# Lower halves of the feed-forward down weights: a negated cast on ScalarE and an accumulating DMA in place of VectorE's subtraction

## What is computed

```python
D_FF = 2816
def swiglu(h, w_gate, w_up, w_down):
    return (jax.nn.silu(h @ w_gate) * (h @ w_up)) @ w_down
# second block, each of two layers
h = rms_norm(x, ffn1_norm[layer])
x = x + FFN_RES * swiglu(h, ffn1_w_gate[layer], ffn1_w_up[layer], ffn1_w_down[layer])
...
h = rms_norm(x, ffn2_norm[layer])
x = x + FFN_RES * swiglu(h, ffn2_w_gate[layer], ffn2_w_up[layer], ffn2_w_down[layer])
# third block
h = layer_norm(DEEPNORM_ALPHA * h + 0.5 * swiglu_3(h, ffn1_w_gate, ffn1_w_up, ffn1_w_down), ln1_g, ln1_b)
```

## Time and profile before

| | us |
|---|---|
| three runs | 3847.56, 3848.74, 3849.88 |
| median | 3848.74 |
| span of the profiled execution | 3845.6 |
| PE busy | 3347.3 |
| DVE busy | 2220.4 |
| ACT busy | 1078.6 |
| POOL busy | 1030.5 |

### The profile page before, as it was taken

The page is one execution under the profiler, slowest core; times in us unless marked ns, Lnnn a source line. Parts: engine busy times, 40 slices in busy tenths (PEclk is TensorE's granted clock), DMA queues, the critical chain, the costliest instruction groups (busy, mean ns, idle before and its releaser), DMA issues. The chain is left out here.

```text
span 3845.6 us, 39174 instructions
## 1 busy us (share of the span) xinstructions
PE 3347.3 (87%) x14474; PEld 2392.3 (62%) x14474; DVE 2220.4 (58%) x3763; ACT 1078.6 (28%) x1659; POOL 1030.5 (27%) x1092
## 2 busy tenths in 40 slices
PE   6997577778997567778999999999999999999998
PEld 4773222224774222223888888887788888887887
DVE  5678766645559766654646555547545435554644
ACT  0212111111212111111434444434443412434342
POOL 0027777764016777775000000000000000200000
PEclk9899899999899899999999999999999999999999
DMA  9459999999738999999652455543455534243453
GB/s 364 173 213 374 409 409 409 409 409 363 269 145 331 409 409 409 409 409 368 201 189 83 143 187 174 186 149 110 153 186 170 186 130 135 87 154 126 150 191 115
DMA packets 402059, 951.47 MB, mean 247 GB/s; under 512 B 30652, under 2 KB 171488, under 8 KB 401632
## 3 DMA queue, kind: packets, MB, share of 16 engines
q0 software_dynamic: 147456, 536.94, 35.5%
q1 hardware_dynamic: 245088, 397.09, 30.9%
q10 hardware_dynamic: 9344, 15.22, 1.1%
HBM read 948.06 MB, written 1.07 MB: 247 GB/s over the span
## 5 line engine op out<-in xcount | busy, mean ns | idle before, releaser
L1505 PE MATMUL PS<-v_rows,xn 128*128 128x512 f32 x1944 | 911.8, 614 | 358.7 <-DMA v_rows<-in_peer_v_dram,peer_ids 351.6
L1505 PEld LDWEIGHTS PS<-v_rows,xn 128*128 128x128 f32 x1944 | 357.8, 194 | 911.5 <-issue 566.7
L1587 DVE CUSTOM_DVE_ANT_0 u_rows<-u_rows,PS 128x1024 f32<-128x1024 f32 x512 | 622.3, 1221 | 367.7 <-DMA u_rows<-in_peer_u_dram,peer_ids 339.3
L796 DVE TENSOR_TENSOR ring_lo<-ring,ring_hi 128x2048 fp32r<-128x2048 f32 x198 | 453.0, 2293 | 260.2 <-ACT ring_hi L735 259.8
L1661 POOL DMA_INDIRECT u_rows<-in_peer_u_dram,peer_ids x512 | 483.6, 945 | 268.3 <-issue 146.1
L1661 POOL DMA_INDIRECT v_rows<-in_peer_v_dram,peer_ids x512 | 487.7, 953 | 169.3 <-issue 142.5
L735 ACT CAST ring_hi<-ring 128x2048 fp32r<-128x2048 f32 x198 | 376.9, 1913 | 245.6 <-PE PS L649 156.3
L649 PE MATMUL PS<-ring_hi,hT_hi 128*128 128x512 f32 x1056 | 418.0, 396 | 5.9 <-DVE hT_lo L830 4.6
L649 PE MATMUL PS<-ring_hi,hT_lo 128*128 128x512 f32 x1056 | 412.4, 391 | 0.0
L649 PE MATMUL PS<-ring_lo,hT_hi 128*128 128x512 f32 x1056 | 412.0, 390 | 0.0
L1565 ACT ACTIVATE xn<-cst,xn 128x128 f32<-128x128 f32 x486 | 161.5, 391 | 725.0 <-PE PS L1505 677.0
(11 more groups left out here) (434 smaller groups left out, 4403.6 us busy)
## 6 DMA issues: line engine op xcount, KB each, us to landing
ring<-in_ffn_w_gate_dram SPq DMA_DIRECT2D x132, 512.0 KB, 4.0
ring<-in_ffn_w_up_dram SPq DMA_DIRECT2D x132, 512.0 KB, 5.0
ring<-in_ffn_w_down_dram SPq DMA_DIRECT2D x66, 1024.0 KB, 4.9
ring<-in_w_in_dram SPq DMA_DIRECT2D x64, 1024.0 KB, 5.1
ada_ring<-in_ada_w_dram SPq DMA_DIRECT2D x96, 512.0 KB, 8.8
ring<-in_peer_wq_dram SPq DMA_DIRECT2D x16, 1024.0 KB, 8.1
ring<-in_c_w_in_dram SPq DMA_DIRECT2D x14, 1024.0 KB, 5.0
ring<-in_w_out_dram SPq DMA_DIRECT2D x8, 1024.0 KB, 12.0
```

The lines of the kernel that those rows point to most:

```text
L796: nc.vector.tensor_tensor(halves(c)[1], slot, halves(c)[0], ALU.subtract).then_inc(S.w_lo, 1)
L1505: ins = nc.tensor.matmul(self.PS[:, 2 * b + h, :], diag[:, r % NDIAG, :], rowsV[:, m % VRING, h * BANK:(h + 1) * BANK], start=(n % (slots ...
L1587: ins = nc.vector.tensor_tensor_reduce(rowsU[:, m % URING, :], rowsU[:, m % URING, :], H[b], 1.0, 0.0, ALU.mult, ALU.add, dots[:, e:e + 1])
```

## The change

The lower half of a down chunk is no longer made by DVE. ACT, right after the cast of the upper half, writes the negated value, rounded to fp32r, into the slot of `ring_lo`. GpSimd then issues a DMA that adds the landed float32 chunk to that slot; the sum is the value minus its upper half. PE waits for that DMA by one of two semaphores, for even and for odd steps. The lower halves of the up chunks stay with DVE and count on a semaphore of their own (`up_lo`; `ups(c)` is the number of up chunks before chunk `c`). In plain stages GpSimd does the power of the norm first and then the eleven DMAs; in stages with a layer norm the eleven DMAs come first.

```diff
+            def ups(c):
+                return c if c < 2 else 2 + (c - 2) // 3 * 2 + (c - 2) % 3
             def up(pe, c, i, parity, half, head=False):
-                pe.wait_ge(S.w_lo, count(c + 1, i, 3 * WINDOWS))
+                pe.wait_ge(S.up_lo, count(ups(c) + 1, i, 2 * WINDOWS))
...
             def down(pe, s, c, i, first=False):
-                pe.wait_ge(S.w_lo, count(c + 1, i, 3 * WINDOWS))
+                pe.wait_ge(down_odd if s % 2 else down_even, count(16 * (s // 2 + 1), i, 8 * WINDOWS))
                 pe.wait_ge(S.hid_lo, count(s + 1, i, WINDOWS))
...
                     nc.scalar.copy(halves(c)[0], self.ring[:, (base + c) % RING, :]).then_inc(S.w_hi, 1)
+                    if c == last or c > 2 and c % 3 == 1:
+                        nc.scalar.activation(halves(c)[1], self.ring[:, (base + c) % RING, :], ACT.Copy, scale=-1.0).then_inc(S.down_neg, 1)
...
-                    nc.vector.tensor_tensor(halves(c)[1], slot, halves(c)[0], ALU.subtract).then_inc(S.w_lo, 1)
+                    nc.vector.tensor_tensor(halves(c)[1], slot, halves(c)[0], ALU.subtract).then_inc(S.up_lo, 1)
...
-                    for c in (3 * s + 4, 3 * s + 5):
-                        if c <= last:
-                            lo(c, i)
+                    if 3 * s + 5 < last:
+                        lo(3 * s + 5, i)
...
             def _(pool):
+                if not layer_norm:
+                    self.norm_gpsimd(pool, S)
+                for s in range(FF_STEPS):
+                    c = min(3 * s + 4, last)
+                    pool.wait_ge(S.down_neg, s + 1)
+                    nc.gpsimd.dma_start(halves(c)[1], self.ring[:, (base + c) % RING, :], accum_op=ALU.add).then_inc(
+                        down_odd if s % 2 else down_even, 16)
                 if layer_norm:
                     self.layer_norm_gpsimd(pool, S)
-                else:
-                    self.norm_gpsimd(pool, S)
```

More of the change, by code:

```diff
@@ L619, in ffn @@
         with ExitStack() as ctx, self.stage(
-                "n_ms n_rstd n_tr hT_hi hT_split w_hi w_lo silu_done hid_ready hid_turned hid_hi hid_lo first_out l_mu l_ms l_rstd", name) as (block, S):
+                "n_ms n_rstd n_tr hT_hi hT_split w_hi up_lo down_neg silu_done hid_ready hid_turned hid_hi hid_lo first_out l_mu l_ms l_rstd", name) as (block, S):
             silu = self.sb("silu_gate", [P, NB, FF_COLS], ctx=ctx)
@@ L629, in ffn @@
             WINDOWS = 4
+            down_even, down_odd = (nc.alloc_semaphore(f"down_lo_{parity}_{name}") for parity in ("even", "odd"))
             if layer_norm:
```

## The result

The changed kernel takes **3865.65 us** (median of 6 runs, 3860.01 to 3875.79), the kernel before 3848.34 us beside it (6 runs, 3841.62 to 3853.78): a ratio of **1.0049, 95% interval 1.0034 to 1.0064**. It is slower by 17 us, more than twice the 0.2% that a measurement here can tell from no change. The profiled execution took 3860.01 us, the shortest of the six.

What follows compares the result with a forecast made beforehand. PE was taken to bound the kernel. A 10.0 us DMA path against 6.7 or 7.0 us in six windows 0 adds 19.2 us to the 3845.6 us span, plus 3.1 for the median: 3868 us, range 3846 to 4030.

Steps and rivals of the forecast that it cites:

- What bounds: In the feed-forward PE sets the pace, 16.82 us per window; removing 151.3 us of DVE subtractions gains 0 on the path.
- The time the DMA has: From negated cast to PE's use: 6.7 us in window 0 (7.0 in layer-norm stages), 12.2 us from window 1 on.
- The time the DMA needs: Issue, landing, second read and delay by a neighbouring load of a down chunk's accumulating DMA: 10.0 us.
- GpSimd's instruction: Issuing the accumulating DMA on GpSimd takes 0.95 us, as for a gather, counted ahead of the landing.
- transfer of 1 MB: The down chunk's DMA takes 4.9 us from issue to landing, as for a plain 1 MB load.
- second read: The accumulate must also fetch its destination, one more megabyte at 409 GB/s: 2.6 us.
- load beside it: SP's load for chunk 2's slot starts with window 0's accumulate and delays it 1.6 us, ends 0 and 3.3.
- The sum: PE waits in six windows 0, 3.3 us in four stages and 3.0 in two: 19.2 us; other windows 0.
- The clock: PE waits of 3 us in window 0 should cost no clock, as the retrieval layer keeps 0.98.
- Hidden anyway: Rival, chance 0.25: window 0's transfer takes 5.9 us, at most 8.0; time 3848.7, up to 3856 us.
- DMA as the bound: Rival, chance 0.28: slow accumulate passes 12.2 us, so every down chunk is late; 4028 us, or up to 4365.
- Faster: Rival, chance 0.04: freed DVE time shortens PE's waits in heads and tails, 11.7 us in all; 3837 us.

Runs made afterwards that it cites:

- plain copy: Changed kernel with a plain DMA copy in place of the accumulating one, leaving the subtraction out; 3847.22 us in one run, against 3849.5 for the kernel before.
- load held back: Changed kernel, but SyncE issues chunk 8's load only after window 0's accumulating DMA has landed; 4004.76 us against 4001.69 for the kernel before, ratio 1.0016.

## Why the prediction was right, step by step

**What bounds.** PE, in every window; a cheaper VectorE and a fuller ScalarE are worth nothing and cost nothing, within 0.1%. The freed 151 us came as forecast (151.5), and so did the gain of 0.

**The time the DMA has.** 6.7 us were forecast for window 0 and 6.7 are measured, though the negated cast took 1.92 us instead of 1.85: the casts and PE both came some 0.9 us earlier than in the trace of before. Windows from 1 on had 12.2 us forecast, and the wait in them is nearly zero, as said. The margin was smaller than the prediction made it look: three of the transfers landed after 11.5 to 11.9 us instead of 8.8 to 9.3. Two of them made the matmul of PE wait for 0.3 us and the third for 0.07, and with the wait of the weight load each put the down chunks back by 0.4 to 0.6 us. GpSimd's timeline shows one of these:

```profile
1966.38 0.87 POOL L887 DMA_DIRECT2D ring_lo<-ring  x1 [16.50 <-ACT ring_lo L742]
```

The cast ahead of it ended at 1965.53, so the instruction began 0.85 us after it, not 0.3. It is no accident of one execution: all three traces of the changed kernel have it in the same three places, in window 7 of the first stage, window 2 of the second and window 6 of the fourth. With the two casts swapped GpSimd is as late there (0.7 to 0.85 us), and the transfers land after 8.1 to 8.2 us. Why it is late at these places, and why the late start costs so much of the landing, was not found.

**The time the DMA needs.** This term was mis-sized, by 1.0 us of 10.0 in the first stage and by 1.2 to 1.3 in the others. Each piece of it can now be set against a run:

| piece | forecast us | measured us | from |
|---|---|---|---|
| GpSimd's instruction | 0.95 | 0.3 | lag behind the cast; the instruction itself lies within the landing |
| transfer of 1 MB | 4.9 | 4.2 | least landing of the plain copy |
| second read | 2.6 | 3.0 | accumulate less copy, least landings: 7.2 less 4.2 |
| load beside it | 1.6 | 1.4 to 1.6 | load held back |
| sum | 10.0 | 9.0 (8.7 to 8.8 in five stages) | cast's end to PE |

The step that failed in this term is the fixed part: it put GpSimd's 0.95 us ahead of a landing that already counts it, and took the landing of a load from HBM for that of a transfer inside SBUF, 5.85 us where 4.5 were measured. The second read was too cheap by 0.4 us, so the errors partly cancel. The Trainium skill, "Collectives: The Full Stack", Part 3, has the reduce limited by its two source reads and not by the addition; no run here separates the two, and the engine time grew by a factor of 1.7 (5.8 over 3.5 us) rather than 2. By its rate one transfer would keep the engines busy for an estimated 4.2 us; the measured 5.8 us are more, so that the 9.1 us that the prediction worked out by it for the whole path came close by luck. What the Trainium skill says in "DMA: Bandwidth & Descriptors", section "Issuing engines are not separate DMA queues", that transfers started by different engines share the same DMA engines, agrees with the load held back: the GpSimd transfer lands 1.4 to 1.6 us sooner without SyncE's load beside it.

**The sum.** 19.2 us of waiting were forecast in six places. Six places it was, with 1.6 to 2.1 us of idle time each instead of 3.0 and 3.3, and two small ones that were not forecast: 13.7 us in all with their slower starts. The profiled span is 6.6 us below the one forecast (3858.2 against 3864.8), of which 1.6 us are the slow stretch in the trace of before and the rest is mostly these smaller waits. The median is only 2.4 us below the forecast, since the changed kernel's medians lie 16 to 22 us above those of before, and that closeness is luck: two errors cancel. The waits were sized too large, and a step of the sum was wrong.

**The clock.** The prediction put at nothing what a wait costs in clock, because PE keeps 0.98 in the retrieval layer while it is busy only 73 of 100 us. That average didn't carry over. Behind 9 of 30 waits of some 2 us in window 0 the granted clock was 0.50 for some eight matmuls, at 1.6 us each. Two such stretches in an execution, which is about the mean of the five traces, make an estimated 3 us; with the 14.2 to 14.6 us of the waits and what follows them that is 17 to 18 us, and the medians show 16 to 22.

**The rivals.** *Hidden anyway* needed a landing under 8.0 us in all. That is the plain copy (4.2 to 5.2 us, no wait); the accumulate, at 8.7 to 9.0 us from the end of the cast, misses it by up to one us. *DMA as the bound* was not reached at a share of 0.90; one accumulate more per window reached it, at 145 us. The 12.2 us that decide it were passed by three single transfers, by 0.2 to 0.4 us. *Faster* is refuted from two sides: with the subtractions left on VectorE and with 60 of them gone, the time is that of before. The bound by the DMA engines was nearer than the reads alone (5.1 us) let expect: an accumulate took 5.8 of the 6.9 us that the loads leave free in a window.

## What to carry to other kernels

Work that moved from an engine with slack to an asynchronous path gained nothing in a stretch bound by PE; all it could do was lose. So such a path has to be held against the shortest time between the last input and the first use. Here that is the first window of a stage (6.7 us), not the steady one that fills the averages (12.2 us). If it does not fit there, start it earlier before giving it up: here the exchange of two casts on one engine was worth the whole loss. And a short wait of PE can cost more than its length, as the slow stretches behind some of these waits show.

## What the runs showed of the hardware that was not expected

- An accumulating DMA inside SBUF costs more than the traffic table tells: for 1 MB it holds the 16 engines for 5.8 us instead of 3.5, lands after 7.2 us at least instead of 4.2, and its issue on GpSimd takes 0.87 us instead of 0.54, with the same bytes counted.
- It makes others late: the 1 MB load of the down weights beside it landed after 9.8 us in the median, 4.9 before and 7.0 beside a plain copy. Nobody waited for that here.
- In the same three windows of every trace of the changed kernel such a transfer is issued 0.4 to 0.55 us late and lands after 11.4 to 11.9 us in place of 9; the cause stayed open. The transfer of the last down chunk of a plain stage lands after 11.3 to 12.3 us in each of these traces, where PE comes 14.9 us after the cast.
- A wait of PE of about 2 us can be followed by some eight matmuls at a granted clock of 0.50 (1.2 GHz), one every 0.43 us: 9 of 30 waits were, and each such stretch cost 1.6 us more.
- A wait of PE costs 0.26 us more than the idle time that the matmul's row shows (2.36 against 2.10 us), since matmuls overlap by 0.16 us and the first one after a wait is 0.1 us slower (0.50 against 0.39 us).
